# Moving the attention half of the output product from the mixing phase into the retrieval phase of a hybrid decoder step

## What is computed

```python
xn = rmsnorm(x, norm_mix)
q, k, v, u = split(xn @ w_in + b_in)            # 512 | 128 | 128 | 512 columns
attn = window_attention(rope(q), rope(k), v)    # window 128, sinks
ssm  = s5_mixer(u)                              # scan, GELU, sigmoid GLU
mix  = concat([rmsnorm(attn, norm_attn_out), rmsnorm(ssm, norm_ssm_out)])
x    = x + mix @ w_out                          # w_out: 1024 x 1024
ffn  = peer_ffn(rmsnorm(x, norm_ffn))           # 8 heads x 16 experts of 16384 per token,
x    = x + ffn                                  # rows of u_table, v_table gathered by index
y    = rmsnorm(x, norm_final)
```

## Time and profile before

| | us |
|---|---|
| median of 3 runs | 3224.87 (3223.51 to 3225.18) |
| profiled execution, its own time | 3225.49 |
| its span in the trace | 3223.7 |
| PE busy / DVE busy / POOL busy | 2266.3 / 2074.2 / 1356.8 |
| first gather issued | 422.19 |

### The profile page before, as it was taken

The page is one execution under the profiler, slowest core; times in us unless marked ns, Lnnn a source line. Parts: engine busy times, 40 slices in busy tenths (PEclk is TensorE's granted clock), DMA queues, the critical chain, the costliest instruction groups (busy, mean ns, idle before and its releaser), DMA issues.

```text
span 3223.7 us, 28170 instructions
## 1 busy us (share of the span) xinstructions
PE 2266.3 (70%) x7579; PEld 783.2 (24%) x7579; DVE 2074.2 (64%) x5164; ACT 942.2 (29%) x3204; POOL 1356.8 (42%) x1266
## 2 busy tenths in 40 slices
PE   8999878866765577557756675667566856685676
PEld 4556543311211122112211221112111211121121
DVE  4446577787568656865676567656765676567654
ACT  3223244333223322232223222322232223222222
POOL 1232034444444444444444444444444444544442
PEclk9999988878887888788878797778688878897799
DMA  5224589999999999999999999999999999999998
GB/s 198 81 76 96 199 324 391 372 421 410 422 421 418 412 414 421 421 414 413 421 408 416 414 421 415 419 409 421 421 414 407 421 414 422 412 421 414 422 418 334
DMA packets 187983, 1207.98 MB, mean 375 GB/s; under 512 B 26600, under 2 KB 34328, under 8 KB 47360
## 3 DMA queue, kind: packets, MB, share of 16 engines
q0 software_dynamic: 157344, 1142.99, 86.3%
q1 hardware_dynamic: 30480, 63.21, 5.6%
HBM read 1190.30 MB, written 15.42 MB: 374 GB/s over the span
## 4 chain that ended last, share of the span: by engine, by line
DMA 38%; PE 26%; issue 8%; DVE 7%; ACT 5%; POOL 4%; another core or an unknown queue 0%; POOLq 0%; DVEq 0%; ACTq 0%
DMA uv_ring<-in_uv_table,idx 38%; PE ACC L2179 16%; PE ZS L2099 5%; DVE uv_ring L1973 4%; POOL uv_ring L1552 3%; ACT dg L1697 2%; PE ZS L2074 1%; ACT dot L1690 1%; PE ZS L2130 1%; ACT dot L1677 1%; PE ZS L2060 0%; PE TQ L2156 0%; PE ZS L2156 0%; DVE S L1989 0%; DVE xn_next L1981 0%
## 5 line engine op out<-in xcount | busy, mean ns | idle before, releaser
L2179 PE MATMUL ACC<-uv_ring,dg 128*64 128x512 f32 x4352 | 1442.2, 773 | 906.4 <-ACT dg L1697 905.3
L1552 POOL DMA_INDIRECT uv_ring<-in_uv_table,idx x1088 | 1260.8, 1159 | 1517.8 <-PE ACC L2179 1300.0
L1973 DVE CUSTOM_DVE_ANT_0 uv_ring<-uv_ring,xn 128x1024 f32<-128x1024 f32 x1088 | 1329.5, 1226 | 836.1 <-DMA uv_ring<-in_uv_table,idx 824.3
L2179 PEld LDWEIGHTS ACC<-uv_ring,dg 128*64 128x64 f32 x4352 | 341.0, 164 | 1936.3 <-ACT dg L1697 1380.5
L1677 ACT ACTIVATE dot<-dot 128x2 f32<-128x2 f32 x544 | 110.6, 203 | 1860.3 <-DVE dot L1973 1847.8
L1697 ACT ACTIVATE dg<-stack,dot 128x64 f32<-128x64 f32 x1088 | 324.1, 340 | 17.7
L1690 ACT ACTIVATE dot<-gate,dot 128x1 f32<-128x1 f32 x1088 | 261.1, 287 | 18.9
L2099 PE MATMUL ZS<-score_w,xnT 128*128 128x512 f32 x512 | 242.3, 614 | 0.0
L518 PE MATMUL PJ<-w_in,xc 128*128 128x512 f32 (+1 forms) x384 | 141.0, 523 | 1.3 <-DVE pj L407 1.3
L2099 PEld LDWEIGHTS ZS<-score_w,xnT 128*128 128x128 f32 x512 | 92.8, 192 | 153.8 <-issue 153.8
L1973 DVE DVE_READ_ACCUMULATOR2_ANT dot<- 128x1 f32 x1088 | 89.1, 82 | 0.0
(11 more groups left out here) (354 smaller groups left out, 1584.3 us busy)
## 6 DMA issues: line engine op xcount, KB each, us to landing
uv_ring<-in_uv_table,idx POOLq DMA_INDIRECT x1088
score_w<-in_w_query SPq DMA_DIRECT2D x8, 1024.0 KB, 18.6
w_in<-in_w_in SPq DMA_DIRECT2D x8, 640.0 KB, 8.7
xt<-in_x SPq DMA_DIRECT2D x9, 512.0 KB, 4.8
xr<-scratch_x SPq DMA_DIRECT2D x9, 512.0 KB
xc<-in_x_columns SPq DMA_DIRECT2D x8, 512.0 KB, 3.8
out_y<-S SPq DMA_DIRECT2D x8, 512.0 KB
scratch_u<-pj SPq DMA_DIRECT2D x9, 256.0 KB, 2.1
```

Source lines behind the costliest of these rows:

```text
L1552: pool.indirect_dma_start(out=ring[:, s_ % RING, :], out_offset=None, in_=a["uv_table"], in_offset=bass.IndirectOffsetOnAxis(ap=idx[:, s_: ...
L1973: V.tensor_tensor_reduce(row, row, xn[:, g, :], 1.0, 0.0, ALU.mult, ALU.add, dot[:, s_:s_ + 1]).then_inc(dots, 1)
L2179: ins = nc.tensor.matmul(ACCS[t % 2][GT * g:GT * (g + 1), b, :], dg[:, n % DG, :], ring[:, n % RING, D + 512 * b:D + 512 * b + 512], start ...
```

## The change

The product with `w_top` leaves mixing. Mixing stores the transposed attention (256 KB a tile) in a DRAM scratch `aT`, in place of `x1`; its root factors stay on the chip in `rsa`. `w_top` is loaded once, in the SSM phase, and stays. Retrieval loads `xr` from the input `x` and the tile's `aT` from scratch. PE makes the product in two halves: for tile 0 before everything else of that phase, for tile 1 at slots 2 and 5 of tile 0's turn, for the others at slots 1 and 5 (`top_product`); DVE adds it to `xr` in slot 10 (`add_attention`; (0, 8) for tile 0). The second `w_bot` half moves from (2, 3) to (2, 4), the sum on DVE from (2, 6) to (2, 8), the normalised tile from (2, 12) to (2, 13). In mixing three of the four early matmuls of `project(t + 1, 2, ...)` take the place where `mix` stood. The `aT` of tile t + 2 is loaded by SyncE (SP) into `xnT` once the last scores of tile t + 1 are made. SP's order of loads and stores changes. To make room, the reserved space for descriptors of POOL's DMAs shrinks to 2048 bytes a partition, and `ex` and `first_cid` share other tiles' space.

PE in mixing:

```diff
                     if not first:
-                        mix(t - 1)
+                        project(t + 1, 2, range(0, 3))
                         sum_squares(t - 1)
...
-                    early = range(0, KD if first else KD // 2)
                     if not first:
-                        project(t + 1, 2, early)
+                        project(t + 1, 2, range(3, KD // 2))
```

SP in mixing:

```diff
-                    x1_out.mark(sp.dma_start(s["x1"][bass.ts(t, P), :], xk[p][:]))
+                    aT_out.mark(sp.dma_start(s["aT"][bass.ts(t, P), :], aT[:].rearrange("p r n -> p (r n)")))
...
+                store_attention(PT - 1)
                 sp.wait_ge(kept, 16 * 3)
                 u_out.held(sp, PT)
+                aT_out.held(sp, PT - 1)
```

```diff
                 early.load(sp, a)
+                early.load_top(sp, a)
...
-                pe.wait_ge(ev["scaled_7"], 1)
...
                 for n, i in enumerate(Y_ORDER):
                     if n == 2:
-                        pe.wait_ge(ev["x1"], 1)
+                        pe.wait_ge(ev["ms"], 1)
```

SP in retrieval:

```diff
+                aT_in.mark(sp.dma_start(z_and_cid[:], s["aT"][0:P, :]))
                 load_queries(0)
...
-                for t in range(PT - 1):
+                for t in range(PT):
                     load_xr(t + 1)
-                    load_y(t + 2)
-                    out(t, P)
-                load_xr(PT)
+                    if t > 0:
+                        out(t - 1, P)
+                    if t < PT - 1:
+                        load_y(t + 2)
+                    if t > 0:
+                        out_landed(t - 1)
+                    if t < PT - 1:
+                        load_attention(t + 2)
```

DVE in retrieval:

```diff
+                    if at == (0, 8) and t == 0 or at == (1, 10) and t > 1:
+                        add_attention(t)
...
-                    elif at == (2, 6):
+                    elif at == (2, 8):
                         k["bot_done"].of(dve, t)
-                        xr_in.of(dve, t)
+                        k["top_added"].of(dve, t)
...
-                    elif at == (2, 12):
+                    elif at == (2, 13):
```

PE in retrieval, and the program's own set-up:

```diff
+                def top_product(t, b):
+
+                    if b == 0:
+                        aT_in.of(pe, t)
+                        k["xr_done"].of(pe, t - 1)
+                        k["xn_taken_a"].of(pe, t - 1)
+                        if t == 0:
+                            pe.wait_ge(early.top_in, 16)
+                        elif t > 1:
+                            k["zb_done"].of(pe, t)
+                    ins = product(t, b, attention(t), w_top)
...
+                    if t == 0 and at in ((0, 1), (0, 2)):
+                        top_product(t, j - 1)
+                    elif t > 1 and at in ((1, 1), (1, 5)):
+                        top_product(t, j // 4)
...
-                    elif at in ((2, 1), (2, 3)):
+                    elif at in ((2, 1), (2, 4)):
...
-    nc = bacc.Bacc("TRN2", target_bir_lowering=False, num_devices=1)
+    nc = bacc.Bacc("TRN2", target_bir_lowering=False, num_devices=1, dynamic_dma_scratch_size=2048)
```

More of the change, by code:

```diff
@@ L242, in step @@
                     if not first:
[L243 to L246, removed]
+                        store_attention(t - 1)
                     store_u(t + 1, 1 - p)
@@ L544, in sum_squares @@
                     k["summed"].mark(ins)
-                def mix(t):
-                    pe.wait_ge(late, 16 * 2)
-                    k["aT_done"].of(pe, t)
-                    k["pj_done"].of(pe, t + 1)
-                    for b in range(2):
-                        for j in range(AW // P):
-                            ins = nc.tensor.matmul(PJ[:, b, :], aT[:, j, :], w_top[:, j, 512 * b:512 * b + 512],
-                                                   start=(j == 0), stop=(j == AW // P - 1))
-                    k["mixed"].mark(ins)
                 def step(t, p, first, last):
@@ L1179, in _ @@
                 tell(dve, "h_sample")
-                dve.wait_ge(ev["mixed"], 1)
+                dve.wait_ge(ev["squares"], 1)
                 ts(ms, XS, 1.0 / AW, EPS, ALU.mult, ALU.add).then_inc(ev["ms"], 1)
-                dve.wait_ge(xr_in, 16)
-                dve.wait_ge(ev["rstd"], 1)
-                for b in range(2):
-                    row = xr[:, 512 * b:512 * b + 512]
-                    ins = nc.vector.scalar_tensor_tensor(row, MO[:, b, :], rstd, row, ALU.mult, ALU.add)
-                ins.then_inc(ev["x1"], 1)
                 def take_outputs(n, i):
@@ L1339, in _ @@
                 pe.wait_ge(ev["one"], 1)
-                for r in range(REP):
-                    nc.tensor.matmul(XS, sqT[:, r, :], one[:], start=(r == 0), stop=(r == REP - 1))
-                for b in range(2):
+                pe.wait_ge(ev["summed_7"], 1)
+                for lo in (0, R):
                     for r in range(REP):
-                        ins = nc.tensor.matmul(MO[:, b, :], aT[:, r, :], w_top[:, r, 512 * b:512 * b + 512],
-                                               start=(r == 0), stop=(r == REP - 1))
-                ins.then_inc(ev["mixed"], 1)
+                        ins = nc.tensor.matmul(XS[lo:lo + R], sqT[:, r, :], one[:], start=(r == 0), stop=(r == REP - 1))
+                ins.then_inc(ev["squares"], 1)
                 pe.wait_ge(ys_copied, 8)
@@ L1382, in retrieve_experts @@
         keys, w_glu, y, b_glu, ident, half = early.keys, early.w_glu, early.y, early.b_glu, early.ident, early.half
+        w_top, rsa = early.w_top, early.rsa
         w_bot = c.sb("w_bot", [P, SW // P, D])
@@ L2190, in retrieve @@
                         for s_ in range(b, b + BATCH):
+                            if turn == "first" and s_ in FIRST_TOP[:2]:
+                                top_product(1, FIRST_TOP.index(s_))
                             for prep in prepared(turn, t, s_):
@@ L2257, in host_layout @@
     rows[:SEQ] = f["x_prompt"].reshape(SEQ, D)
-    rows[SEQ:SEQ + NS_ROWS] = f["x_sample"].reshape(NS_ROWS, D)
+    rows[SEQ:SEQ + P] = np.tile(f["x_sample"].reshape(NS_ROWS, D), (2, 1))
     pos = np.zeros(ROWS_PAD, np.float32)
```

166 lines of the change are left out of this document (81 added, 85 removed).

## The result

The changed kernel takes 3207.92 us (median of 5 runs, 3206.44 to 3209.19); the kernel before took 3224.87 (3223.51 to 3230.34) beside it. The ratio is 0.9943, with a 95% interval of 0.9932 to 0.9953: faster by 17 us, where 40 were forecast, and outside the range that ended at 3203.

What follows compares the result with a forecast made beforehand. Mixing was taken as bound by PE, retrieval by its gathers. Terms -38.4 + 0.6 - 1.6 + 7.2 - 2.5 - 5.7 = -40.4 from 3225.49 gave 3185.1, less 0.6 for the median: 3184.5 us; range 3168 to 3203, over 8 in 10.

Steps and rivals of the forecast that it cites:

- Mixing: Mixing steps 1 to 7: 38.4 us gained without the `w_top` product; 0.6 us added waiting for the last `aT` store.
- SSM phase: SSM phase: 1.6 us gained before the sample scores and SSM outputs, less low-clock losses after PE's gaps; bounds 0 and 4.8.
- Opening: Opening of retrieval: tile 0's product lands on the path, so the first gather comes 7.2 us later; bounds 3.5 and 13.7.
- PE's bursts in the turns: Turns 1 to 7: two bursts of 8 records (3.5 us) at slots 1 and 5, hidden, costing nothing.
- `aT` loads: Turns 1 to 7: 256 KB more DMA in each, 0.62 us each, 4.3 us in all.
- DVE's additions: Turns 1 to 7: 1.4 us of DVE at slot 10 in each, costing nothing.
- Descriptor space: POOL's gathers in retrieval: with at most eight under way, the smaller space costs nothing.
- The later sum steps: Turns 1 to 7: DVE's wait at slot 24 and its dip go; about 11 us in all, 10 taken.
- Later sum steps: Tile 0's turn: they give back about 4 us; with DVE's 1.5 us exposed, net -2.5.
- the forecast for the turns: Retrieval's turns: net -2.5 us in tile 0's turn and -5.7 us in turns 1 to 7.
- Rival B: Retrieval terms go against it: dips stay (+10), opening costs 10 to 13, tile 0's turn loses; 3193 to 3213, chance 0.16.
- The prediction's own signs of being wrong: PE idle in mixing steps 4 to 6, first gather after 395, or slots 6 to 18 of turns below 415 GB/s.

Runs made afterwards that it cites:

- e2: Changed kernel with descriptor space back at 16384 bytes a partition and `w_top` cut to one block, 256 KB loaded instead of 2 MB: 3206.61 us.
- e3: Changed kernel with each half of the attention product one matmul instead of four for tiles 2 to 8: 3207.91 us.
- e5: Kernel before with 64 unused bytes a partition ahead of `uv_ring`: 3237.85 us, ratio 1.0037 to before.
- e12: Changed kernel with `nmax` (32 bytes a partition) moved ahead of the ring, which then starts at a multiple of 256: 3166.04 us, ratio 0.9815 to before.
- e6: Kernel before with 352 unused bytes a partition ahead of `uv_ring`, which then starts at a multiple of 512: 3197.19 us, ratio 0.9917 to before.
- e11: Changed kernel with the `aT` loads of tiles 2 to 8 cut from 256 KB to 32 KB: 3204.63 us.
- e1: Kernel before with only the descriptor space cut to 2048 bytes a partition: 3228.58 us, ratio 1.0008 to before.
- e4: Kernel before with only the later second `w_bot` half, sum and normalised tile: 3223.99 us, ratio 0.9988 to before.
- e7: Changed kernel with `stack` and `nmax` (288 bytes) moved ahead of the ring, which then starts at a multiple of 512: 3168.12 us, ratio 0.9821 to before.
- e14: e12 with the second `w_bot` half, sum and normalised tile back at their former places: 3169.80 us, ratio 0.9827 to before.
- e13: Kernel before with the second `w_bot` half moved to (2, 4) and the sum left at (2, 6): 3241.45 us, ratio 1.0053 to before.

## Why the prediction was wrong

Step by step, from the profiled executions:

- **Mixing, -38.4 and +0.6: right.** 242.14 - 282.43 = -40.3, where -37.8 was forecast. Steps 4 to 6 take 24.4 us (24.8 predicted), steps 1 to 3 26.0 to 26.1 (26.5 predicted) with PE waiting before X as foretold, and step 7 hangs on DVE. The prices per step were a little low.
- **SSM phase, -1.6: wrong sign, small.** From 242.14 to the phase's end at 336.95 it takes 94.8 us, where it was 375.4 - 282.4 = 93.0: +1.8. The prediction reckoned PE's gaps and the low clock after them; on PE this came to a gain, of 0.6 us. It had no term for the load of `w_top`, behind which SP's rows grew. With 256 KB of it (e2) the phase takes 334.31 - 242.38 = 91.9 us, 1.0 less than before.
- **Opening, +7.2: right.** 389.90 - 336.95 = 52.95 us, where it was 422.19 - 375.4 = 46.8: +6.2. The product ran 9.01 us and the GLU product got the fast clock. The wait for `xr` that the bound named came true in part (2.11 us before the GLU product).
- **The first gather, by luck.** The prediction's terms put it at 422.19 - 38.4 + 0.6 - 1.6 + 7.2 = 390.0 (it wrote "about 389"), and it came at 389.9. Three misses cancel in that: -2.5 us in mixing, +3.4 in the SSM phase, -1.0 in the opening. In sum, all of the error lies behind it.
- **PE's bursts in the turns, 0: right** (e3).
- **`aT` loads, +4.3, and DVE's additions, 0: not contradicted.** With the ring at the same place, turns 1 to 7 take 5.9 us more in the changed kernel than in e5 (2295.5 and 2289.5) and 5.4 more in e12 than in e6 (2258.2 and 2252.8). Both terms lie in that, and e11 (3.3 of an expected 3.8) agrees with the loads' price without showing it.
- **Descriptor space, 0: right** (e1, e2).
- **The failed step: "The later sum steps: ... its wait, and with it the dip, goes ... of which I take 10" and "Later sum steps should give back about 4 us".** The wait and the dip went; the 14 us did not come. e4 has 2.6 us by the medians, and in the traces 1.8 from its first gather to its end: 1.9 in tile 0's turn and nothing in turns 1 to 7. GB/s missing in a window were taken for lost time. Only about half of them were idle engines (5.4 us, not 11), and most of that came back as idle engines at other slots. 14 - 1.8 = 12.2 us of the error are this. Why it comes back stays open.
- **What no term held: the address of the ring.** 64 bytes of root factors shifted the gathers' target and made each of them 0.010 us longer: 9.4 us from first gather to end in e5, 11.5 by its medians (3237.85 - 3226.33).

12.2 + 9.4 = 21.6 of the 22.9 us between the forecast for the turns (-8.2) and their measure (+14.7) are accounted for. The address alone carries the time past the range's end: without 9.4 us it would, by that estimate, be 3198.5. Rival B named the range that came true (3193 to 3213) by luck. Its dips that stay went, its costly opening did not come about, and it did not know of the address; only its guess that the lost time would move and not go fits. The prediction's own signs of being wrong did not show this: PE did not idle in steps 4 to 6, the first gather came before 395, and 1725 to 1740, early in tile 4's turn, moved 419 GB/s (by slots 6 to 18, one turn of seven had 413).

One reading of the earlier trace rows is off, though nothing hangs on it: from the eleventh slice the line stands at 407 to 422, not 402 to 423, and in the first ten at 76 to 421, not 53 to 399. And 1.6 us for the SSM phase follows from no sum; its terms give 1.4 to 2.0.

With the address out of the way the change is worth more than it showed: e7 against e6 is 29 us by the medians, after against e5 30.

The best kernel here is e12, 3166.04 us: the change with one 32-byte tile moved ahead of the ring, 42 us (1.3%) under the changed kernel and 1.85% under the one before.

## What to carry to other kernels

When a tile is added or resized, look at where the big DMA targets behind it come to lie: in a kernel that is bound by 8 KB gathers, the start of the ring at a multiple of 256 bytes was worth 1.4 to 1.8% of their rate, more than the change under study, and it costs one moved tile. Do not price a dip in the GB/s by its area: count from the packets how much of it is idle engines, and take the stall out in an experiment before counting on it. Here 5.4 us of idle engines in seven turns were worth nothing when taken away, while 14 us more cost their full size. Compare stretches in which none of the changed work runs: a difference there is one of placement.

## What the runs showed of the hardware

- Gathers of 128 rows of 8 KB take 2.450, 2.483 and 2.493 us each with the target at 0, 160 and 224 bytes past a multiple of 256 (e12, before, after), and each of their 8 KB packets 309, 314 and 315 ns.
- A space of 2048 bytes a partition for descriptors carried eight such gathers as well as 16384 did (e1, e2).
- DVE stalls of 1.5 to 2.8 us a turn could be taken away without gain in turns 1 to 7 (before, e4; the same at another place of the ring, e14, e12); stalls of 4.5 us cost 2.1 us a turn (e13).
- Behind the 2 MB load of `w_top` two stores took SP 4.03 us to issue, where it took 1.48 with 256 KB (after, e2), and the phase ended 2.6 us later.
